# Last head's key tiles: transposed by VectorE and moved through DRAM instead of by TensorE and ScalarE; Pool's two last-head steps swapped; third output block's evacuations spread over four chunks

## The chip, the cores and the metric

One core of one Trainium2 chip runs the whole kernel. The metric is the device time of one execution in microseconds (us). The kernel before took 1402.96 us, the median of 3 runs (1402.95, 1402.96 and 1403.58).

## What is computed

The reference is one inference step of a mixer layer. 640 tokens (128 of context, 512 latent) of 2048 features are normalised, scaled and shifted, and multiplied by one input projection of nine parts of 1024 columns. Eight heads of retention and eight heads of a gated linear recurrence (HGRN2) read the parts, forward and backward, and write final states. Both branches go through one output projection, a gated residual and a last norm. What matters here is how the recurrence's state takes up the keys of a chunk, and the output projection:

```python
s = (jnp.exp(b_last[:, :, 0, :])[..., None] * s
     + jnp.einsum('bhjd,bhjv->bhdv', kc * jnp.exp(b_last - b), vc))
...
out = jnp.concatenate([o_r, o_h], axis=-1).astype(x.dtype) @ w_out
x = x + (gate[:, None, :] * out).astype(x.dtype)
```

The keys times their decay factors are called the factored keys below. The einsum sums over the tokens j, so TensorE needs the tokens of the factored keys on the partitions, while the kernel computes them with the features there: every head's factored keys have to be transposed.

## The kernel before, in words

All loops are written out by hand for five instruction streams (SP issues DMAs, ScalarE is ACT, VectorE is DVE, Pool is GpSimd, TensorE is PE), and semaphores order them: each engine runs its own list from top to bottom, and an instruction whose semaphore isn't there yet holds up all behind it on that engine. Nothing is scheduled by a tool; the written order is the order of the chip.

**Heads.** Each of eight heads streams its input-projection weights in 18 chunks of 512 KB. ACT rounds a chunk to its high part (`split`, L730), DVE makes the low part (L1202), and PE multiplies high by high, high by low and low by high (for token parts L2130 to L2132). The recurrences of head h - 1 are interleaved with the chunks of head h. At the end of a head DVE runs, in `items(17, h, ...)`: the first level's decay differences (`differences`, L1472 and L1474), `boundary_decays` (L1419, L1420), `query_factors` (L1446, twice), `tokens_last` (L1329, which copies two PSUM banks of projected tokens away and so frees them for PE), and `turn_keys` (L1437 to L1439, three transposes of 32x32 blocks). Pool makes the factored keys (`key_factors`, L1824, one 128x1280 product, after ACT's exponentials in L920) and multiplies key decays of a level (`key_decay`, L1847 and L1848, after ACT's exponentials in L879). For heads 0 to 6 the factored keys then go through DRAM: SP's `move_keys` waits for `turn_keys`, writes 512 KB (L536), waits for that, and reads it back in four pieces (L541), which completes the transpose; PE's `chunk_updates` (L2220, L2222) multiplies the result with the values.

**The last head** has no following head, so its recurrences are interleaved with the first block of the output projection. PE's list there is (L2329 on): the first weight chunk for tiles 0 to 3, `level_scores` 0 (L2147), retention updates (L2174, L2175), more of the block, `level_scores` 1, retention outputs (L2186 to L2189), `level_scores` 2, the second weight chunk, and then `key_tokens`: eight 128x128 transposes of the factored keys (L2206, L2208) into two PSUM banks. ACT's `keys` (L863, L864) copies them to `kltok`, PE does the first chunk for tile 4, and `chunk_updates` follows. The first matmul of the block waits for DVE's `tokens_last`, and `level_scores` 3 for DVE's `chunk_states` (L1484, L1486). Pool does `key_decay(last, 0)` before `key_factors(last)`.

**Output projection.** `w_out` is taken in four blocks of 512 columns by 8 chunks; a chunk is split by ACT (L1030) and DVE (L1662) into one of two weight slots, and PE multiplies (L2314 to L2316). A block has five token tiles of 512 columns in five PSUM banks. While block nb runs, DVE evacuates block nb - 1 (`finish`, per tile a gate product L1722 and a residual addition L1729): two tiles after the split of chunk 1 and three after that of chunk 2. ACT then squares a tile (L1064) in each of chunks 3 to 7, and Pool multiplies it by the norm's weights (L1909). In the fourth block (nb = 3) PE does only three of the five tiles in its first pass, so a chunk there is 18 matmuls long and not 30.

Of the kernel before, what the change touches and what calls it, by code (L numbers as in the profile page):

```python
# [41 lines left out]
HEADS = 8  # L42
# [82 lines left out]
def layer(nc, x_prompt, x_sample, s_ret_f, s_ret_b, s_hg_f, s_hg_b, c, c_ctx,  # L125
# [3 lines left out]
    with ctx:  # L129
# [196 lines left out]
        last_keys, pe_hu, pe_level = Signal("last_keys", 2), Signal("pe_hu"), Signal("pe_level", PRODUCTS)  # L326
# [129 lines left out]
        def _(sp):  # L456
# [39 lines left out]
            def store_states(h, new_f, new_b, buf, ready, stored):  # L496
                sp.wait_ge(ready.sem, ready.at(h))
                for s, new in enumerate((new_f, new_b)):
                    sp.dma_start(new[0, 0, bass.ds(h, 1)].rearrange("h d v -> (h d) v"), buf[:, s, :]).then_inc(stored.sem, 16)
# [141 lines left out]
            load_w_out(2)  # L641
            store_states(last, n_ret_f, n_ret_b, rst, r_state, r_state_stored)
# [60 lines left out]
        def _(act):  # L703
# [156 lines left out]
            def keys(h):  # L860

                act.wait_ge(last_keys.sem, last_keys.at(0, 1))
                act.activation(kltok[:, 0:4, :], tiles(ps[:, C, :]), ACT.Copy)  # L863
                act.activation(kltok[:, 4:8, :], tiles(ps[:, DD, :]), ACT.Copy).then_inc(last_keys.sem, 1)  # L864

# [177 lines left out]
            keys(last)  # L1043
# [69 lines left out]
        def _(dve):  # L1113
# [552 lines left out]
            own_decay(last, 0)  # L1666
            split_w(1)
# [114 lines left out]
            for m in range(WCHUNKS, OUT_CHUNKS):  # L1782
                nb, j = m // WCHUNKS, m % WCHUNKS
                split_w(m)
                if nb < OUT_BLOCKS:
                    if j == 1:
                        finish(nb - 1, 0, 2)
                    if j == 2:
                        finish(nb - 1, 2, TILES)
                else:  # L1790

                    if j == 0:
                        finish(OUT_BLOCKS - 1, 0, 1)
                    if j == 1:
                        finish(OUT_BLOCKS - 1, 1, EARLY)
                    if j == 2:
                        early_norm()
                        finish_right(0)
                        finish_left(0)
                        partial_variances()  # L1800
                    if j >= 4:
                        finish_right(j - 3)
# [15 lines left out]
        def _(pool):  # L1818
# [77 lines left out]
            last = HEADS - 1  # L1896
            key_decay(last, 0)
            key_factors(last)
# [18 lines left out]
        def _(pe):  # L1917
# [282 lines left out]
            def key_tokens(h):  # L2200

                pe.wait_ge(h_kl.sem, h_kl.at(h))
                pe.wait_ge(r_S.sem, r_S.at(h))
                pe.wait_ge(r_state.sem, r_state.at(h))
                for i, t in enumerate((0, 1, 2, 3)):
                    nc.tensor.transpose(ps[:, C, tile_cols(i)], KL[:, 0, tile_cols(t)], ident)  # L2206
                for i, t in enumerate((0, 2, 3, 4)):
                    ins = nc.tensor.transpose(ps[:, DD, tile_cols(i)], KL[:, 1, tile_cols(t)], ident)  # L2208
                ins.then_inc(last_keys.sem, 1)

            def chunk_updates(h):

                if h == HEADS - 1:
                    pe.wait_ge(last_keys.sem, last_keys.at(0))
                else:
                    pe.wait_ge(k_moved.sem, k_moved.at(h))
                    pe.wait_ge(r_S.sem, r_S.at(h))
                    pe.wait_ge(r_state.sem, r_state.at(h))
# [125 lines left out]
            pe.wait_ge(r_scaled.sem, r_scaled.at(last))  # L2344
            key_tokens(last)
            pe.wait_ge(h_sT.sem, h_sT.at(last, 3))
            for kk in range(WK):
                first_block(0, kk, shared)
            chunk_updates(last)
# [183 lines left out]
```

## Time and profile before

| what | value |
|---|---|
| median of 3 runs | 1402.96 us |
| the profiled execution's own time | 1402.7 us |
| its span, first to last instruction | 1400.9 us |
| mean granted TensorE clock | 0.998 |
| PE busy | 1384.3 us, 99% |
| DVE, ACT, POOL busy | 1001.1, 483.5 and 367.9 us |
| share of PE in the chain that ended last | 96% |

The span is shorter than the execution's own time by what lies around the first and last instruction (1.8 us). Matmuls overlap: the mean of one is 0.39 us, but one of 512 columns starts every 0.227 us when PE runs without a gap, so gaps are read from the distance of two starts, not from the busy share.

### The profile page before, as it was taken

Reading aid. Unit: us, or ns where it says so; the run is one execution under the profiler, and the core shown is the slowest. Engines: PE = TensorE matmul, PEld = TensorE weight load, DVE = VectorE, ACT = ScalarE, POOL = GpSimd, SP = SyncE. Lnnn points to the kernel's source line nnn. Section 1 sums busy time; section 2 is a strip of 40 time slices with the busy share of each in tenths; the row PEclk is TensorE's granted clock in tenths of the full one; section 3 lists DMA queues with packets and bytes.
Section 4 is the critical chain, followed back from the end, with each engine's and each line's share of the span. In section 5 each row is a group of like instructions: output and inputs, shape, how many; then the busy total and the mean of one; then the engine's idle time right before and its main releaser. Section 6 shows DMA issues by size and latency. Waiting matters only on the chain.

```text
span 1400.9 us, 24706 instructions
## 1 busy us (share of the span) xinstructions
PE 1384.3 (99%) x10042; PEld 1166.2 (83%) x10042; DVE 1001.1 (71%) x1330; ACT 483.5 (35%) x842; POOL 367.9 (26%) x292
## 2 busy tenths in 40 slices
PE   7999999999999999999999999999999999999997
PEld 5788898889888988898889888988898888888886
DVE  5655676667689888988888888877676768532345
ACT  4323243233333333342334333333333344221234
POOL 0000114311532153215321532153206225201220
PEclk9999999999999999999999999999999999999999
DMA  9995443435354535444444444433433357182235
GB/s 388 418 393 184 118 126 71 117 73 140 86 169 114 168 96 175 111 154 119 160 116 140 122 159 126 130 97 106 113 98 85 105 155 274 52 306 94 90 106 210
DMA packets 207735, 212.40 MB, mean 152 GB/s; under 512 B 144256, under 2 KB 156816, under 8 KB 202768
## 3 DMA queue, kind: packets, MB, share of 16 engines
q1 hardware_dynamic: 207600, 210.89, 47.8%
q8 instruction: 79, 1.29, 0.4%
q14 instruction: 24, 0.20, 0.0%
q10 hardware_dynamic: 32, 0.02, 0.0%
HBM read 182.27 MB, written 24.40 MB: 148 GB/s over the span
## 4 chain that ended last, share of the span: by engine, by line
PE 96%; DMA 2%; DVE 1%; SPq 0%; issue 0%; ACT 0%; DVEq 0%; ACTq 0%
PE ps L2130 10%; PE ps L2132 10%; PE ps L2131 10%; PE ps L1968 9%; PE ps L1970 8%; PE ps L1969 8%; PE ps L1944 8%; PE ps L2314 5%; PE ps L2316 5%; PE ps L2315 5%; DMA area<-in_w_mod 2%; PE ps L2147 2%; PE ps L1975 2%; PE ps L1976 2%; PE ps L1977 2%; PE ps L1934 2%
## 5 line engine op out<-in xcount | busy, mean ns | idle before, releaser
L1202 DVE TENSOR_TENSOR w_lo<-area,w_hi 128x1024 fp32r<-128x1024 f32 x143 | 190.4, 1331 | 208.0 <-ACT w_hi L730 207.9
L730 ACT ACTIVATE w_hi<-area 128x1024 fp32r<-128x1024 f32 x143 | 151.5, 1059 | 485.9 <-PE ps L2132 255.7
L2130 PE MATMUL ps<-w_hi,hT_hi 128*128 128x512 f32 x640 | 250.6, 392 | 0.0
L2131 PE MATMUL ps<-w_lo,hT_hi 128*128 128x512 f32 x640 | 249.2, 389 | 0.0
L2132 PE MATMUL ps<-w_hi,hT_lo 128*128 128x512 f32 x640 | 249.1, 389 | 0.0
L1968 PE MATMUL ps<-hT_hi,w_hi 128*128 128x512 f32 x512 | 204.9, 400 | 0.5 <-DVE hT_lo L1262 0.4
L1970 PE MATMUL ps<-hT_hi,w_lo 128*128 128x512 f32 x512 | 199.8, 390 | 0.0
L1969 PE MATMUL ps<-hT_lo,w_hi 128*128 128x512 f32 x512 | 199.8, 390 | 0.0
L2132 PEld LDWEIGHTS ps<-w_hi,hT_lo 128*128 128x128 f32 x640 | 120.2, 188 | 25.2
L2131 PEld LDWEIGHTS ps<-w_lo,hT_hi 128*128 128x128 f32 x640 | 120.2, 188 | 24.6
L2130 PEld LDWEIGHTS ps<-w_hi,hT_hi 128*128 128x128 f32 x640 | 120.2, 188 | 24.6
L1836 POOL TENSOR_TENSOR area<-area 128x320 f32<-128x320 f32 x56 | 49.5, 884 | 320.3 <-PE ps L2147 261.7
L2314 PE MATMUL ps<-w_hi,hT_hi 128*128 128x512 f32 x296 | 116.7, 394 | 0.4 <-DVE w_lo L1662 0.3
L1968 PEld LDWEIGHTS ps<-hT_hi,w_hi 128*128 128x128 f32 x512 | 96.1, 188 | 24.6 <-issue 4.1
L2316 PE MATMUL ps<-w_hi,hT_lo 128*128 128x512 f32 x296 | 115.4, 390 | 0.0
L2315 PE MATMUL ps<-w_lo,hT_hi 128*128 128x512 f32 x296 | 115.3, 389 | 0.0
L1970 PEld LDWEIGHTS ps<-hT_hi,w_lo 128*128 128x128 f32 x512 | 96.1, 188 | 20.8
L1969 PEld LDWEIGHTS ps<-hT_lo,w_hi 128*128 128x128 f32 x512 | 96.2, 188 | 18.5
L1662 DVE TENSOR_TENSOR w_lo<-area,w_hi 128x1024 fp32r<-128x1024 f32 x32 | 42.1, 1317 | 95.6 <-ACT w_hi L1030 95.5
L1460 DVE SCALAR_TENSOR_TENSOR gate_sums<-gate_raw,small,gate_sums 128x512 f32<-128x512 f32 x128 | 102.1, 858 | 3.1 <-DMA gate_raw<-in_w_gate 3.1
L879 ACT ACTIVATE area<-area 128x1280 f32<-128x1280 f32 x56 | 70.6, 1272 | 88.8 <-DVE area L1474 84.4
L1847 POOL TENSOR_TENSOR area<-area 128x320 f32<-128x320 f32 x56 | 67.0, 1197 | 92.7 <-ACT area L879 92.7
(282 smaller groups left out, 2429.1 us busy)
## 6 DMA issues: line engine op xcount, KB each, us to landing
area<-in_w_in SPq DMA_DIRECT2D x144, 512.0 KB, 4.4
area<-in_w_mod SPq DMA_DIRECT2D x26, 1024.0 KB, 12.1
area<-in_w_out SPq DMA_DIRECT2D x38, 512.0 KB, 3.7
gate_raw<-in_w_gate SPq DMA_DIRECT2D x32, 512.0 KB, 4.2
gate_raw<-in_w_mod SPq DMA_DIRECT2D x6, 1024.0 KB, 12.3
o_hi_scratch<-area SPq DMA_DIRECT2D x56, 80.0 KB, 2.4
o_lo_scratch<-area SPq DMA_DIRECT2D x56, 80.0 KB, 2.4
hT_hi<-o_hi_scratch SPq DMA_DIRECT2D x14, 320.0 KB, 7.1
```

The costliest lines, as they stand in the source:

```text
L730: act.activation(split_weights(h, n)[0], raw[:, n % 3, :], ACT.Copy).then_inc(wt_hi.sem, 1)
L1202: v.tensor_tensor(lo, raw[:, n % 3, :], hi.bitcast(F32), ALU.subtract).then_inc(wt_lo.sem, 1)
L1944: ins = mm(ps[:, (banks.start, banks.stop - 1)[s], 0:HALF], wt[:, w], x[:, k, s * HALF:(s + 1) * HALF], start=k == 0 and step == 0, stop=k ...
L1968: mm(ps[:, bank, :], w_hi[:, n % 2, w], hT_hi[:, k, P:T], start=k == 0, stop=False)
L1969: mm(ps[:, bank, :], w_hi[:, n % 2, w], hT_lo[:, k, P:T], start=False, stop=False)
L1970: return mm(ps[:, bank, :], w_lo[:, n % 2, w], hT_hi[:, k, P:T], start=False, stop=k == KT - 1)
L2130: mm(out, hT_hi[:, k, tile_cols(t)], w_hi[:, n % 2, w], start=k == 0, stop=False)
L2131: mm(out, hT_hi[:, k, tile_cols(t)], w_lo[:, n % 2, w], start=False, stop=False)
L2132: i = mm(out, hT_lo[:, k, tile_cols(t)], w_hi[:, n % 2, w], start=False, stop=k == KT - 1)
L2314: mm(out, hT_hi[:, k, tile_cols(t)], hi, start=k == first, stop=False)
L2315: mm(out, hT_hi[:, k, tile_cols(t)], lo, start=False, stop=False)
L2316: return mm(out, hT_lo[:, k, tile_cols(t)], hi, start=False, stop=k == final)
```

## The change

Four edits. DVE turns the last head's keys too: `turn_keys(last)` stands after `own_decay(last, 0)`, ahead of the split of the second `w_out` chunk. SP calls `move_keys(last)` after it has issued the third `w_out` chunk, ahead of the retention states' store. PE's `key_tokens` and ACT's `keys` are gone; `chunk_updates(last)` waits for the DMA like that of the other heads. Pool does `key_factors(last)` before `key_decay(last, 0)`. And DVE evacuates the third output block (nb = 2, during block 3) as two tiles after chunk 1, and one each after chunks 2, 3 and 4. Line numbers of the changed file differ from those of before by up to 16.

```diff
@@ SP @@
             load_w_out(2)
+            move_keys(last)
             store_states(last, n_ret_f, n_ret_b, rst, r_state, r_state_stored)
@@ ACT @@
-            def keys(h):
-
-                act.wait_ge(last_keys.sem, last_keys.at(0, 1))
-                act.activation(kltok[:, 0:4, :], tiles(ps[:, C, :]), ACT.Copy)
-                act.activation(kltok[:, 4:8, :], tiles(ps[:, DD, :]), ACT.Copy).then_inc(last_keys.sem, 1)
...
             decays(last, 2)
-            keys(last)
             split_w(2)
@@ DVE @@
             own_decay(last, 0)
+            turn_keys(last)
             split_w(1)
...
                 if nb < OUT_BLOCKS:
+                    late = nb == OUT_BLOCKS - 1
                     if j == 1:
                         finish(nb - 1, 0, 2)
                     if j == 2:
-                        finish(nb - 1, 2, TILES)
+                        finish(nb - 1, 2, 3 if late else TILES)
+                    if late and j in (3, 4):
+                        finish(nb - 1, j, j + 1)
@@ Pool @@
             last = HEADS - 1
+            key_factors(last)
             key_decay(last, 0)
-            key_factors(last)
@@ PE @@
-            def key_tokens(h):
-
-                pe.wait_ge(h_kl.sem, h_kl.at(h))
-                pe.wait_ge(r_S.sem, r_S.at(h))
-                pe.wait_ge(r_state.sem, r_state.at(h))
-                for i, t in enumerate((0, 1, 2, 3)):
-                    nc.tensor.transpose(ps[:, C, tile_cols(i)], KL[:, 0, tile_cols(t)], ident)
-                for i, t in enumerate((0, 2, 3, 4)):
-                    ins = nc.tensor.transpose(ps[:, DD, tile_cols(i)], KL[:, 1, tile_cols(t)], ident)
-                ins.then_inc(last_keys.sem, 1)
-
             def chunk_updates(h):
 
-                if h == HEADS - 1:
-                    pe.wait_ge(last_keys.sem, last_keys.at(0))
-                else:
-                    pe.wait_ge(k_moved.sem, k_moved.at(h))
-                    pe.wait_ge(r_S.sem, r_S.at(h))
-                    pe.wait_ge(r_state.sem, r_state.at(h))
+                pe.wait_ge(k_moved.sem, k_moved.at(h))
+                pe.wait_ge(r_S.sem, r_S.at(h))
+                pe.wait_ge(r_state.sem, r_state.at(h))
...
             first_block(1, 1, own)
-            pe.wait_ge(r_scaled.sem, r_scaled.at(last))
-            key_tokens(last)
             pe.wait_ge(h_sT.sem, h_sT.at(last, 3))
             for kk in range(WK):
                 first_block(0, kk, shared)
+            pe.wait_ge(r_scaled.sem, r_scaled.at(last))
             chunk_updates(last)
```

Three places of the built programs follow. Nearly every SBUF buffer of the recurrences lies in one tensor, `area`; `ps` is PSUM. On **Pool**, at the end of the loop over the heads, before (L1824 is `key_factors`, L1847 and L1848 are `key_decay`, L1836 and L1837 are `differences`):

```order
L1894 COMPARE_AND_BRANCH
L1847 TENSOR_TENSOR area<-area 128x5x64
L1848 TENSOR_TENSOR area<-area 128x5x64
L1824 TENSOR_TENSOR area<-area 128x1280
L1836 TENSOR_TENSOR area<-area 128x10x32
L1837 TENSOR_TENSOR area<-area 128x10x32
```

and with the change:

```order
L1892 COMPARE_AND_BRANCH
L1822 TENSOR_TENSOR area<-area 128x1280
L1845 TENSOR_TENSOR area<-area 128x5x64
L1846 TENSOR_TENSOR area<-area 128x5x64
L1834 TENSOR_TENSOR area<-area 128x10x32
L1835 TENSOR_TENSOR area<-area 128x10x32
```

The 128x1280 product of the factored keys has moved ahead of the first level's two key-decay products. On **PE**, after the second weight chunk of the first output block, before (L2206 and L2208 are the transposes, L2220 and L2222 are `chunk_updates`):

```order
L2316 MATMUL ps<-w_hi,hT_lo 128x512
L2206 MATMUL ps<-con,area 128x128 x4
L2208 MATMUL ps<-con,area 128x128 x4
L2314 MATMUL ps<-w_hi,hT_hi 128x512
L2315 MATMUL ps<-w_lo,hT_hi 128x512
L2316 MATMUL ps<-w_hi,hT_lo 128x512
L2314 MATMUL ps<-w_hi,hT_hi 128x512
L2315 MATMUL ps<-w_lo,hT_hi 128x512
L2316 MATMUL ps<-w_hi,hT_lo 128x512
L2220 MATMUL ps<-area 128x128 x4
L2222 MATMUL ps<-area 128x128 x4
```

and with the change:

```order
L2300 MATMUL ps<-w_hi,hT_lo 128x512
L2298 MATMUL ps<-w_hi,hT_hi 128x512
L2299 MATMUL ps<-w_lo,hT_hi 128x512
L2300 MATMUL ps<-w_hi,hT_lo 128x512
L2298 MATMUL ps<-w_hi,hT_hi 128x512
L2299 MATMUL ps<-w_lo,hT_hi 128x512
L2300 MATMUL ps<-w_hi,hT_lo 128x512
L2204 MATMUL ps<-area 128x128 x4
L2206 MATMUL ps<-area 128x128 x4
```

Eight transposes have left the list, and nothing has taken their place. On **DVE**, in chunks 1 to 4 of the fourth output block (splits L1662, gate products L1722, additions L1729), before:

```order
L1722 TENSOR_TENSOR area<-ps,area 128x512 x2
L1729 TENSOR_TENSOR area<-area 128x512 x2
L1662 TENSOR_TENSOR w_lo<-area,w_hi 128x1024
L1722 TENSOR_TENSOR area<-ps,area 128x512 x2
L1729 TENSOR_TENSOR area<-area 128x512
L1722 TENSOR_TENSOR area<-ps,area 128x512
L1729 TENSOR_TENSOR area<-area 128x512 x2
L1662 TENSOR_TENSOR w_lo<-area,w_hi 128x1024 x5
```

and with the change:

```order
L1717 TENSOR_TENSOR area<-ps,area 128x512 x2
L1724 TENSOR_TENSOR area<-area 128x512 x2
L1656 TENSOR_TENSOR w_lo<-area,w_hi 128x1024
L1717 TENSOR_TENSOR area<-ps,area 128x512
L1724 TENSOR_TENSOR area<-area 128x512
L1656 TENSOR_TENSOR w_lo<-area,w_hi 128x1024
L1717 TENSOR_TENSOR area<-ps,area 128x512
L1724 TENSOR_TENSOR area<-area 128x512
L1656 TENSOR_TENSOR w_lo<-area,w_hi 128x1024
L1717 TENSOR_TENSOR area<-ps,area 128x512
L1724 TENSOR_TENSOR area<-area 128x512
L1656 TENSOR_TENSOR w_lo<-area,w_hi 128x1024 x3
```

The third tile's evacuation stays behind the split of chunk 2; those of the fourth and fifth tile now stand behind the splits of chunks 3 and 4.

## Rows read from the trace of the kernel before

**Rows 1.** The page, part 4: shares of the span in the chain that ended last.

```profile
PE 96%; DMA 2%; DVE 1%; SPq 0%; issue 0%; ACT 0%; DVEq 0%; ACTq 0%
```

**Rows 2.** Waits of PE from 1140 us to the end: us in total, times, longest.

```profile
PE ps L2314 <- DVE w_lo L1662: 0.3, 1, 0.3
```

**Rows 3.** Timeline of PE around the transposes: start us, us, engine, line, what, count.

```profile
1173.95 0.39 PE L2316 MATMUL ps<-w_hi,hT_lo 128*128 128x512 f32 x1
...
1175.29 0.39 PE L2315 MATMUL ps<-w_lo,hT_hi 128*128 128x512 f32 x1
```

**Rows 4.** Timelines of DVE and PE: the end of `chunk_states`, and `level_scores` 3.

```profile
1182.62 0.34 DVE L1486 SCALAR_TENSOR_TENSOR area<-area,small,ps 128x128 f32<-128x128 f32 x1
...
1183.16 0.56 PE L2147 MATMUL ps<-area 128*32 128x32 f32 x40
```

**Rows 5.** Timelines of POOL and DVE: end of head 6; last row of head 0.

```profile
1012.31 3.30 POOL L1824 TENSOR_TENSOR area<-area 128x1280 f32<-128x1280 f32 x1 [9.95 <-ACT area L920]
...
1012.31 0.48 DVE L1472 TENSOR_TENSOR area<-area 128x320 f32<-128x320 f32 x1
1012.71 3.24 DVE L1474 TENSOR_TENSOR area<-area 128x320 f32<-128x320 f32 x1
...
1017.62 1.22 DVE L1329 COPY area<-ps 128x1024 f32<-128x1024 f32 x1
...
1019.57 0.54 DVE L1439 STREAM_TRANSPOSE area<-area 128x384 f32<-128x384 f32 x1
...
181.64 3.24 DVE L1474 TENSOR_TENSOR area<-area 128x320 f32<-128x320 f32 x1
```

**Rows 6.** Timelines of ACT, DVE and PE at the end of the last head.

```profile
1150.36 1.26 ACT L920 ACTIVATE area<-area 128x1280 f32<-128x1280 f32 x1
...
1152.04 0.48 DVE L1474 TENSOR_TENSOR area<-area 128x320 f32<-128x320 f32 x1
...
1154.78 1.23 DVE L1329 COPY area<-ps 128x1024 f32<-128x1024 f32 x1 [0.51 <-PE ps L2132]
...
1155.71 0.39 PE L2132 MATMUL ps<-w_hi,hT_lo 128*128 128x512 f32 x1
1156.15 0.47 PE L2314 MATMUL ps<-w_hi,hT_hi 128*128 128x512 f32 x1
```

**Rows 7.** Landing times of L536, L541, L631; timelines of SP and ACT between them.

```profile
DMA to landing us min/median/max: 4.9/5.3/5.9
...
1027.55 2.75 SPq L541 DMA_DIRECT2D area<-key_scratch  x4
...
DMA to landing us min/median/max: 2.8/3.6/4.4
...
1166.12 0.43 SPq L631 DMA_DIRECT2D area<-in_w_out  x1
...
1179.93 1.06 ACT L1030 ACTIVATE w_hi<-area 128x1024 fp32r<-128x1024 f32 x1 [0.42 <-PE ps L2316]
...
DMA to landing us min/median/max: 3.5/3.7/11.0
```

**Rows 8.** Timelines of ACT, DVE and PE in the fourth output block.

```profile
1345.54 1.06 ACT L1030 ACTIVATE w_hi<-area 128x1024 fp32r<-128x1024 f32 x1 [3.02 <-PE ps L2316]
...
1347.49 2.32 DVE L1662 TENSOR_TENSOR w_lo<-area,w_hi 128x1024 fp32r<-128x1024 f32 x1
...
1349.13 0.39 PE L2316 MATMUL ps<-w_hi,hT_lo 128*128 128x512 f32 x1
...
1350.19 0.39 PE L2315 MATMUL ps<-w_lo,hT_hi 128*128 128x512 f32 x1
```

**Rows 9.** Windows, start of the kernel: length, busy us by engine, PEclk, DMA share, GB/s.

```profile
5.00:10.00 5.00, 3.29 (x13) 1.92 (x12) 1.81 (x6) 2.81 (x6) 0.00 (x0) 0.82 0.99 391
10.00:15.00 5.00, 5.00 (x17) 2.90 (x16) 2.48 (x3) 4.64 (x8) 0.00 (x0) 0.84 1.00 414
...
25.00:30.00 5.00, 3.36 (x60) 2.48 (x62) 3.52 (x11) 1.20 (x2) 0.00 (x0) 1.00 1.00 416
```

More of the change, by code:

```diff
@@ L325, in layer @@
         h_sq, h_rms, h_gated = Signal("h_sq"), Signal("h_rms", 2), Signal("h_gated")
-        last_keys, pe_hu, pe_level = Signal("last_keys", 2), Signal("pe_hu"), Signal("pe_level", PRODUCTS)
+        pe_hu, pe_level = Signal("pe_hu"), Signal("pe_level", PRODUCTS)
         pe_ho = Signal("pe_ho")
@@ L2198, in retention_columns, with chunk_updates @@
                 nc.tensor.transpose(ctx_columns(following), sT[:, 0:P], ident).then_inc(pe_columns.sem, 1)
-            def key_tokens(h):
-                pe.wait_ge(h_kl.sem, h_kl.at(h))
+            def chunk_updates(h):
+                pe.wait_ge(k_moved.sem, k_moved.at(h))
                 pe.wait_ge(r_S.sem, r_S.at(h))
                 pe.wait_ge(r_state.sem, r_state.at(h))
-                for i, t in enumerate((0, 1, 2, 3)):
-                    nc.tensor.transpose(ps[:, C, tile_cols(i)], KL[:, 0, tile_cols(t)], ident)
-                for i, t in enumerate((0, 2, 3, 4)):
-                    ins = nc.tensor.transpose(ps[:, DD, tile_cols(i)], KL[:, 1, tile_cols(t)], ident)
-                ins.then_inc(last_keys.sem, 1)
-            def chunk_updates(h):
-                if h == HEADS - 1:
-                    pe.wait_ge(last_keys.sem, last_keys.at(0))
-                else:
-                    pe.wait_ge(k_moved.sem, k_moved.at(h))
-                    pe.wait_ge(r_S.sem, r_S.at(h))
-                    pe.wait_ge(r_state.sem, r_state.at(h))
                 for i, t in enumerate((0, 1, 2, 3)):
```

## The prediction

> **What bounds the kernel now.** I read the chain of waits first: PE is 96% of it [rows 1]. Then PE's own waits: from 1140 us on, where all the edits lie, the profile names a single one, 0.3 us in the fourth output block [rows 2]. So an edit gains only what PE no longer executes, plus that wait, and loses whatever PE must newly wait for. The rest of the reading looks for such waits, in the timelines of all engines around the last head's end (1150 to 1190 us) and in the fourth block (1340 to 1355 us).
>
> **TensorE's transposes go.** The reader is to see the distance of two starts: from the last matmul ahead of the transposes (1173.95) to the second one behind them (1175.29) it is 1.34 us [rows 3]; two starts without anything between are 2 x 0.227 = 0.45. PE is the path, nothing covers this: **-0.89 us**.
>
> What is late next? `level_scores` 3 needs DVE's `chunk_states`, which end at 1182.62 + 0.34 = 1182.96; PE starts those scores at 1183.16, and the part that waits is the last fifth of about 0.5 us, so at 1183.56 [rows 4]. That margin is 0.6 us. DVE's list up to there waits for PE's retention outputs, which stand ahead of the transposes, and for nothing behind them, so it doesn't move with PE. PE now asks at 1183.56 - 0.89 = 1182.67; a signal from DVE to a PE start takes 0.14 us (L1329 ends at 1156.01, PE starts at 1156.15) [rows 6]. 1182.96 + 0.14 - 1182.67 = 0.43: **+0.4 us**, between 0 (if DVE gains a little somewhere) and 0.6.
>
> **Pool's key factors first.** In the last head before, ACT's exponentials end at 1150.36 + 1.26 = 1151.62, and Pool does the 128x1280 product only later, so DVE's L1474 at 1152.04 takes 0.48 us [rows 6]. In the heads before it Pool does that product first, as the change has it: it starts 0.3 to 0.4 us before L1474, and L1474 takes 3.24 us, ending about when Pool does (1012.31 + 3.30 against 1012.71 + 3.24) [rows 5]. So it was at the end of all seven heads, the first and the last of which stand there. The two engines hold each other off. With the change the last head's end has their geometry: Pool starts at about 1151.70, L1474 at 1152.04. Behind L1474 the order on DVE is the same as there; L1329 starts 1017.62 - 1012.71 = 4.91 us after it [rows 5], so at 1156.95 in place of 1154.78, and ends at 1158.17. L1329 frees PSUM banks for the first matmul of the output projection, and PE already stands at it now: it starts 0.14 us after L1329, 0.44 after the matmul before [rows 6]. It moves to 1158.31: **+2.16 us**, with nothing on PE to cover it. The upper bound is 2.76 (3.24 - 0.48, if DVE's 0.51 us wait for PE ahead of L1329 didn't absorb some), the lower bound 0, if the product doesn't hold L1474.
>
> The Trainium skill says of that pair ("SBUF — State Buffer", section "SBUF: two separate sides") that Pool and a VectorE instruction with two SBUF inputs share ports under an exclusive lock, which whichever starts first has for its whole length. Taken to the letter, L1472, which has two such inputs and is under way when Pool is released, would keep Pool off for some 0.4 us, and all that follows would be as much later: by the page the sum below would be +1.5. The rows show Pool and L1472 (0.48 us) starting together at 1012.31 and neither longer than elsewhere [rows 5], so I keep 2.16.
>
> L1474 is 2.76 us late for ACT's exponentials of that level as well, and with them for one product on DVE and two on Pool. PE asks for these in `level_scores` 1, which starts at about 1164.3 (the second weight chunk's 24 matmuls end at 1174.2 [rows 3], so start at 1168.5; some 4 us of outputs and scores stand ahead) and now 2.16 later: hidden, 0.
>
> **DVE turns the keys.** In head 6 the three transposes run from the end of L1329 (1018.84) to 1019.57 + 0.54 = 1020.11: 1.27 us [rows 5]. In the new place they follow L1329 (1158.17) and a product of 0.8 us that may be held by Pool, and end at about 1160.5; the split behind them is done by 1162. PE wants it at 1168.5 + 2.16: 0.
>
> **SP moves the keys.** The write is issued at about 1160.6 and lands in at most 5.9, four reads take 2.75 to issue and at most 4.4 to land [rows 7]: 1160.6 + 5.9 + 2.75 + 4.4 = 1173.7. PE asks in `chunk_updates`, which now stand six matmuls behind the second chunk: before, they began at 1175.29 + 5 x 0.227 = 1176.4, now at 1176.4 - 0.89 + 2.16 = 1177.7. Cover 4.0 us: 0. SP is a queue, and all behind `move_keys` waits with it, at most the 1169.3 - 1160.6 = 8.7 us until its last read is issued: the state store, seven pairs of loads for the block's later half, and a `w_out` chunk that goes from 1166.12 to at most 1174.8 [rows 7]. ACT splits that chunk at 1179.93, now 1.27 later, and landing takes 3.7, at worst 11.0: 1178.5, at worst 1185.8. At the median it is hidden by 2.7 us: 0.
>
> **ACT's two copies** go. ACT next waits for PE there: 0.
>
> **Third block's evacuations.** Two of three tiles leave the gap ahead of the split that ran from 1347.49 to 1349.81. PE's starts around it are 1349.13 and, two on, 1350.19: 1.06 where 0.45 is due [rows 8]. With the change the split waits for ACT alone, which ends at 1346.60; even if it takes 2.32 us again it is done at 1349.0, and PE asks at 1349.36. **-0.61 us**, at least -0.4. In chunks 3 and 4, of 18 x 0.227 = 4.1 us each, DVE has room for one tile beside the split.
>
> **Sum:** -0.89 + 0.43 + 2.16 - 0.61 = +1.1 us. The profiled execution took 1402.7 us, so 1403.8; the median of the runs is 0.26 higher, and against it the forecast is **1404.0 us**: no change that a measurement of this kernel can tell (about 0.2%, 2.8 us).
>
> **Rivals.**
> *The clock falls in the new pause.* PE would stand from 1155.94 to 1158.31, 2.37 us. At the start of the kernel two stretches of 5 us hold 1.7 us of idle PE each: in the one the granted clock fell to the lower level, 1.2 GHz of 2.4 (means of 0.82 and 0.84 there and in the next stretch), in the other it stayed at 1.00 [rows 9]. A fall cost 5 x 0.18 + 5 x 0.16 = 1.7 us. For it: the new pause is longer than either. Against it: PE is fully busy on both sides. Time: 1405.7, or 1405.3 if part of the slow stretch falls into the pause. The Trainium skill's page "TensorE: Matmul & The Clock Gate" (What's actually happening) says that the array is throttled by default and only activity releases it, by which a pause endangers the clock; no row here shows a pause of this length.
> *Pool doesn't hold DVE* in the last head: then +2.16 goes and the rest stays, -1.1: 1401.9. For it only that Pool comes out of its loop there; against it seven heads of seven.
> *The keys come late.* This one ends clearly slower. The decisive point is PE at `chunk_updates`, 1177.7: beyond that each us costs one, and 1.7 us late (1179.4) makes the whole slower by 0.2%. If write and reads both landed as slowly as the slowest `w_out` chunk, 11.0 [rows 7], they would be there at 1160.6 + 11.0 + 2.75 + 11.0 = 1185.4, 7.7 us late: 1411.7. Against it: all seven earlier heads landed within the bounds above.
> *The evacuation edit does nothing* (Pool's products hold a split elsewhere): -0.61 goes, 1404.6.
>
> **Chances:** forecast 0.45, clock 0.32, no hold 0.09, late keys 0.06, evacuations 0.08. The range, **1403.0 to 1406.0**, takes in the forecast with its bounds (a half as long stall gives 1402.9, 0.6 us of `level_scores` wait and a stall of 2.76 give 1404.8), the evacuations and the clock; it leaves out no hold and late keys. Slower by over 0.2% (above 1405.8) are late keys and a third of the clock's cases with its bounds added: 0.19. Faster by over 0.2% is no case, 0.02 for what I don't see. Same: 0.79.
>
> **What would show it.** In the profile after: L1474's counterpart near 1152 us at 3.2 us and not 0.5; L1329's counterpart ending near 1158.2; PE's first output-projection matmul near 1158.3 with an idle of some 2 us put down to DVE; the granted clock of 1158 to 1162; no transposes ahead of `chunk_updates`, and the key pieces landing before 1174; a small wait of PE at `level_scores` 3; no wait in the fourth block. The forecast is wrong if L1474 stays at 0.5 us (then faster), if PE idles at `chunk_updates`, or if the clock shows 0.5 behind the pause.

## The result, and the profile after

The changed kernel took **1404.97 us** (median of 22 runs, 1403.51 to 1406.53), the kernel before 1402.80 us (22 runs, 1402.49 to 1404.07): ratio 1.0014, 95% interval 1.0008 to 1.0020. By the 0.2% named in the prediction that is no change; it is a small loss all the same, 2.2 us, and not the 1.1 us of the sum.

The runs of the changed kernel fall into two groups by their mean granted TensorE clock. Ten show 0.998, their median is 1403.79 us; twelve show 0.995 to 0.997, their median is 1405.65. The first group lies where the forecast put the time; the second, but for its fastest run, where the clock rival put it, and two more profiles below show one execution of either kind. That fastest run is the profiled execution itself: 1404.8 us (span 1403.0), 2.1 more than the one of before. Behind the pause its granted clock is 1.00 in every window up to 1390 us; it is lower from 5 to 15 us (0.81 and 0.84) and from 1395 us on (0.74), as in the profile of before (0.82, 0.84 and 0.74).

The page's chain of the changed kernel, which answers to [rows 1]:

```profile
PE 93%; DMA 5%; DVE 1%; ACT 1%; SPq 0%; issue 0%; DVEq 0%; ACTq 0%
```

PE is still the path; DMA's larger share comes from ahead of all the edits, most of it from the start of the kernel. PE's waits from 1140 us on, which answer to [rows 2]: us in total, times, longest.

```profile
PE ps L2298 <- DVE area L1323: 2.3, 1, 2.3
PE ps L2298 <- DVE w_lo L1656: 0.2, 1, 0.2
```

The wait in the fourth block is gone, and two have come: one for `tokens_last` (now L1323), one for a split of weights (L1656). Both can be followed in the timelines. First the end of the last head on POOL, DVE and PE, which answers to [rows 6] (start us, us, engine, line):

```profile
1152.65 3.23 POOL L1822 TENSOR_TENSOR area<-area 128x1280 f32<-128x1280 f32 x1 [11.13 <-ACT area L915]
...
1152.58 0.48 DVE L1466 TENSOR_TENSOR area<-area 128x320 f32<-128x320 f32 x1
1152.98 3.25 DVE L1468 TENSOR_TENSOR area<-area 128x320 f32<-128x320 f32 x1
...
1157.89 1.22 DVE L1323 COPY area<-ps 128x1024 f32<-128x1024 f32 x1
...
1156.55 0.39 PE L2130 MATMUL ps<-w_hi,hT_lo 128*128 128x512 f32 x1
1159.26 0.47 PE L2298 MATMUL ps<-w_hi,hT_hi 128*128 128x512 f32 x1 [2.32 <-DVE area L1323]
```

Pool starts its long product during L1466, and L1468 behind that takes 3.25 us where it took 0.48. `tokens_last` ends at 1159.11, and PE starts 2.71 us after its last projection matmul; before it was 0.44. **The stall costs 2.27 us.**

Then PE's chunk updates and the weight split behind them (PE, then DVE):

```profile
1178.69 1.05 PE L2204 MATMUL ps<-area 128*128 128x128 f32 x8
...
1182.22 0.50 PE L2298 MATMUL ps<-w_hi,hT_hi 128*128 128x512 f32 x1 [0.19 <-DVE w_lo L1656]
...
1179.63 1.00 DVE L1466 TENSOR_TENSOR area<-area 128x320 f32<-128x320 f32 x1
1180.55 0.48 DVE L1468 TENSOR_TENSOR area<-area 128x320 f32<-128x320 f32 x1
1180.95 1.21 DVE L1656 TENSOR_TENSOR w_lo<-area,w_hi 128x1024 fp32r<-128x1024 f32 x1
```

`chunk_updates` began at 1176.45 before (in the fence below) and begin at 1178.69 now, 2.24 later, after PE had come to the stall 0.84 later (1156.55 against 1155.71) and lost 2.27 in it: 0.84 + 2.27 - 2.24 = **0.87 us won** by the transposes' leaving. Six matmuls of the output projection behind the updates, PE stands for the split of the third `w_out` chunk, which DVE has done only at 1182.16. The start of that matmul comes 0.58 after the one before it, and the next one 0.34 after that, where 0.227 each is due: **0.46 us given back**. The same places before (PE, DVE):

```profile
1176.45 1.10 PE L2220 MATMUL ps<-area 128*128 128x128 f32 x8
...
1179.67 0.39 PE L2314 MATMUL ps<-w_hi,hT_hi 128*128 128x512 f32 x1
...
1177.80 1.23 DVE L1662 TENSOR_TENSOR w_lo<-area,w_hi 128x1024 fp32r<-128x1024 f32 x1
```

There the split ended at 1179.03, and PE asked for it at 1179.67.

In the fourth block (DVE), which answers to [rows 8], the splits have 1.2 us again and stand behind nothing but ACT:

```profile
1349.37 1.23 DVE L1656 TENSOR_TENSOR w_lo<-area,w_hi 128x1024 fp32r<-128x1024 f32 x1 [1.52 <-ACT w_hi L1025]
```

No two starts of PE's matmuls in that block are over 0.30 us apart; the gap of 0.61 is gone.

The sum of what the edits did in this profile is 2.27 - 0.87 + 0.46 - 0.61 = +1.25, and with the 0.84 us by which PE was late before any of them, the 2.1 of the two profiles. These 0.84 are no work of the change: the programs are alike up to there, the same changed program starts that matmul at 1155.59 and 1155.92 in two more profiles, and over all the profiles below it starts anywhere from 1155.2 to 1156.9 us.

### The profile page after: what moved, and what is told of

Its sections match the earlier page's. It is cut to its first block, busy times and chain, and to the rows that moved or that the text cites. A ratio compares the mean times of both kernels' runs of the same rounds, so it can differ in the third digit from the quotient of the medians.

```text
span 1403.0 us, 24697 instructions
## 1 busy us (share of the span) xinstructions
PE 1383.5 (99%) x10034; PEld 1165.2 (83%) x10034; DVE 1004.2 (72%) x1333; ACT 482.4 (34%) x840; POOL 368.7 (26%) x292
## 4 chain that ended last, share of the span: by engine, by line
PE 93%; DMA 5%; DVE 1%; ACT 1%; SPq 0%; issue 0%; DVEq 0%; ACTq 0%
PE ps L2128 10%; PE ps L2129 10%; PE ps L2130 10%; PE ps L1966 8%; PE ps L1967 8%; PE ps L1968 8%; PE ps L1942 8%; PE ps L2298 5%; PE ps L2299 5%; PE ps L2300 5%; DMA area<-in_w_mod 3%; PE ps L2145 2%; PE ps L1973 2%; PE ps L1974 2%; PE ps L1975 2%; PE ps L1932 1%
## 5 line engine op out<-in xcount | busy, mean ns | idle before, releaser
L1656 DVE TENSOR_TENSOR w_lo<-area,w_hi 128x1024 fp32r<-128x1024 f32 x32 | 39.9, 1248 | 93.8 <-ACT w_hi L1025 93.7
```

## Experiments

Three questions are open: whether Pool's order alone makes the stall, whether the clock makes the second group of runs, and why the gains of the two other edits are not kept. Medians are set against the median of the runs of before on the same chip. Since the start of the kernel varies, each profile is also read from the start of PE's last projection matmul to the start of its last matmul, the stretch that holds all the edits ("tail"):

| kernel | tail, us | against before |
|---|---|---|
| before | 236.21 | |
| changed, first profile | 237.48 | +1.27 |
| changed, two more profiles | 238.91, 237.37 | +2.70, +1.16 |
| Pool's order undone | 236.07 | -0.14 |
| Pool's order alone | 238.39 | +2.18 |
| evacuations alone | 235.61 | -0.60 |
| PE kept busy in the pause, ten matmuls twice | 239.06 | +2.85 |
| PE kept busy in the pause, once | 237.27 | +1.06 |
| the pause made longer | 241.23 | +5.02 |
| Pool behind, `tokens_last` first | 236.02 | -0.19 |
| ... and the third split first | 236.33 | +0.12 |
| ... and the last order on DVE | 235.40 | -0.81 |

### Pool's order undone

```diff
-            key_factors(last)
             key_decay(last, 0)
+            key_factors(last)
```

> The change with Pool's two steps in their old order (key_decay(last, 0), then key_factors(last)); all else as changed. Theory (the 128x1280 product on Pool holds DVE's second difference, tokens_last comes late, PE stands 2.3 us): DVE's L1468 takes 0.48 us again, PE's first output-projection matmul starts 0.44 us after the last projection matmul as before, the stall of 2.3 us is gone. Keys are turned when Pool's product ends (about 1159.5 on the time axis of before), transposed by 1161, landed by 1173.5 at worst, PE asks at 1175.6: no wait there. The time is before - 0.89 (transposes) + 0.4 (DVE behind PE in w_out chunk 2 or level_scores 3) - 0.61 (evacuations) = -1.1: 1401.7 us against a median of 1402.8, and the runs lie close together as those of before do. Rival A (DVE's turning and the key DMAs cost the time): it stays near 1405. Rival B (keys late without Pool's head start): PE waits at chunk_updates, each us one.

1402.62 us (11 runs, 1402.16 to 1403.57) against 1402.81: ratio 0.9999, interval 0.9990 to 1.0008; tail -0.14 and not -1.1. The stall is gone (PE starts 0.44 us after its last projection matmul), keys are in time, but 0.9 us of the expected gain are missing. PE's waits of this kernel from 1140 us on, and DVE's transposes in its timeline:

```profile
PE ps L2184 <- DVE area L1374: 0.8, 1, 0.8
PE ps L2298 <- DVE w_lo L1656: 0.2, 1, 0.2
```

```profile
1159.65 0.71 DVE L1431 STREAM_TRANSPOSE area<-area 128x512 f32<-128x512 f32 x1 [2.86 <-POOL area L1822]
...
1165.36 0.34 DVE L1374 SCALAR_TENSOR_TENSOR area<-area,small,ps 128x128 f32<-128x128 f32 x1
```

The theory failed in part: the stall went, and the full gain didn't come. Rival B's wait at `chunk_updates` didn't come either; rival A was wrong in its time, but turning the keys does cost. A new wait stands at the retention outputs (L2184), for `retention_chain` (L1374), which is behind `turn_keys` on DVE, and `turn_keys` itself waits 2.86 us for Pool's product here. Read from the starts, the new wait is worth 0.87 us, and the one for the third chunk's split 0.46, as in the changed kernel. In the changed kernel the last L1374 started at 1166.81 and PE asked at 1168.14, with margin to spare, since PE had been held for 2.3 us. The transposes were hidden by the very stall that the other edit made.

### Pool's order alone

```diff
+            key_factors(last)
             key_decay(last, 0)
-            key_factors(last)
```

> The kernel before with Pool's two steps swapped and nothing else. Theory: L1474 takes 3.24 us, PE's first output-projection matmul is 2.2 to 2.3 us later, all else moves with it: +2.2, 1405.0 us, with the runs spread upward by up to 2.5 us as with the change if that spread comes from the new pause. Rival A (turning and DMAs): no change, 1402.8. Rival C (the spread of the change's runs comes from its DMAs, not from the pause): 1405.0 with all runs within 0.5 us.

1406.01 us (9 runs, 1405.08 to 1407.12): ratio 1.0024, interval 1.0014 to 1.0034. L1474 takes 3.24 us, and PE:

```profile
1158.53 0.47 PE L2314 MATMUL ps<-w_hi,hT_hi 128*128 128x512 f32 x1 [2.20 <-DVE area L1329]
```

PE's last projection matmul started at 1155.93, so the stall is 2.60 - 0.44 = 2.16 us. No last-head key was turned by DVE here and no DMA added: the swap makes the stall by itself. The median is 1.0 above the 1405.0 expected; seven of the nine runs have a mean clock below 0.998, where the changed kernel has 12 of 22. The two runs at a clock of 0.998 or more took 1405.08 and 1405.56, the seven below it 1405.99 to 1407.12, so the spread doesn't come from the key DMAs either.

### The evacuations alone

The edit to `finish` in the kernel before, as in the change.

> The kernel before with the third block's evacuations spread over four chunks and nothing else. Theory: the split of chunk 3 no longer stands behind the evacuation of three tiles, PE's gap at 1349 us (0.61) goes: 1402.2 us. Rival (Pool's products hold a split elsewhere, or a later wait takes the gain): within 0.2 of before, 1402.8.

1402.18 us, 11 runs between 1401.95 and 1402.41, against 1402.81 (31 runs from 1402.31 on). The ratio, 0.9996 with interval 0.9987 to 1.0005, can't tell it from no change, but the profile can: the view of PE's waits from 1140 us on is empty, the matmuls of the fourth block follow each other at 0.227 us, and the tail is 0.60 us shorter, the size of the gap that is gone.

### PE kept busy in the pause

```diff
                     pe.wait_ge(tok_act.sem, tok_act.at(last, 1))
+                    for n in range(10):
+                        mm(ps[:, A, :], hT_hi[:, 15, 0:P], hT_hi[:, 15, P:T], start=True, stop=True)
                     pe.wait_ge(tok_dve.sem, tok_dve.at(last))
```

> The change, with ten more 128x512 matmuls on PE right ahead of its wait for tokens_last (into PSUM bank A, which nothing reads then; the output is not touched), so that PE works through most of its 2.3 us pause. The runs of the change lie in two groups, near 1403.75 and near 1405.6 us. Theory clock (the upper group is a fall of the granted clock set off by the pause): all runs near 1403.8, granted clock 0.998 in all. Rival (the upper group has another cause: start of the kernel, DMAs): the two groups stay, median about 1405. If the ten matmuls outlast the pause, they add up to 0.3 us to either.

1405.60 us (11 runs, 1405.18 to 1406.70), ratio 1.0018, interval 1.0009 to 1.0027. The edit did more than was meant: the code around it runs a second time for the chunk's fifth tile, and ten matmuls more stood on PE's path there (2.27 us), of which 0.46 took the place of the wait for the third chunk's split. 1403.79 + 2.27 - 0.46 = 1405.60. So it can be read as a single group, but not well; the tail, 239.06, comes near the same sum (237.37 + 2.27 - 0.46 = 239.18). Therefore once more, in the first call only:

```diff
+                    if 0 in tokens:
+                        for n in range(10):
+                            mm(ps[:, A, :], hT_hi[:, 15, 0:P], hT_hi[:, 15, P:T], start=True, stop=True)
```

> The change with ten more 128x512 matmuls on PE ahead of its wait for tokens_last, this time once only (the earlier kernel issued them a second time, 2.27 us more, ahead of the first chunk's fifth tile); the output is not touched. Theory clock (the upper group of the change's runs is a fall of the granted clock set off by the 2.3 us pause): all runs within 0.5 us of 1403.8, granted clock 0.998 or above but for a run or two. Rival (the upper group comes from the start of the kernel or from the DMAs): the runs spread from 1403.5 to 1406.5 as the change's do, median near 1405.

1403.94 us, all 11 runs between 1403.42 and 1404.28, ten of them at 0.998 or 0.999: ratio 1.0006, interval 0.9997 to 1.0015. Work that changes nothing in the result, put into the pause, brings the median down by a microsecond, since the second group is gone. (The two medians come from separate sessions; the kernel before took 1402.80 and 1402.83 us in them.) The tail is that of the changed kernel with the clock kept (237.27 against 237.37): PE's real work starts again 2.50 us after its last projection matmul, about as late as without the ten matmuls (2.59), and only the clock is saved.

### The pause made longer

```diff
+                if isinstance(h, int) and h == LAST:
+                    v.tensor_copy(gate_sums[:, :, :], ps[:, 2:4, :])
+                    v.tensor_copy(gate_raw[:, 0, 0:2 * WIDE].rearrange("p (b n) -> p b n", b=2), ps[:, 2:4, :])
                 v.tensor_copy(tok[:, 3:5, :], ps[:, 2:4, :]).then_inc(tok_dve.sem, 1)
```

> The change with two more copies of 1.14 us each on DVE right ahead of tokens_last (the same PSUM banks, copied into buffers that nothing reads any more; the output is not touched), so that PE's pause is 4.6 us and not 2.3. Theory clock: the granted clock falls behind the pause in nearly every run, and the profile shows windows below 1.00 between 1160 and 1175 us; 1403.75 + 2.28 + 1.7 to 2 = 1407.7 to 1408.0. Rival (the pause does nothing to the clock): 1406.0 for half of the runs and up to 1408.5 for others, all windows from 1150 to 1390 us at 1.00.

1408.16 us (5 runs, 1407.65 to 1409.68), ratio 1.0040, interval 1.0026 to 1.0054; no run is above a clock of 0.997. Windows of two us of its PE (length, PE busy and instructions, granted clock, DMA share, GB/s):

```profile
1156.00:1158.00 2.00, 0.55 (x3) 1.00 1.04 390
1158.00:1160.00 2.00, 0.00 (x0) 1.00 1.05 398
1160.00:1162.00 2.00, 0.92 (x3) 0.82 1.04 393
1162.00:1164.00 2.00, 2.00 (x6) 0.50 0.61 229
1164.00:1166.00 2.00, 2.00 (x46) 0.83 0.53 215
```

The clock goes to the lower level behind the pause, as the clock theory said; the median is 0.2 above its range. The parts fit: the tail is 3.86 us longer than that of the changed kernel with the clock kept (241.23 against 237.37), 2.33 of it is the longer pause (4.92 us from start to start, 1156.16 to 1161.08, against 2.59), and 1.53 are left for the fall.

### The changed kernel again, twice

No edit; two more executions, profiled.

> The changed kernel again, for another profile of it. Theory clock: if this execution takes over 1405 us, its granted clock is below 1.00 in windows behind PE's pause, between 1157 and 1170 us, with matmuls 0.43 us apart; if it takes under 1404, the clock stays at 1.00 there. Rival: an execution over 1405 us with 1.00 in all windows there, its extra time ahead of 1150 us.

> The changed kernel once more, with the same expectation as the one before it: over 1405 us with a fall of the granted clock behind the pause, or under 1404 without one.

1405.30 and 1404.05 us, one of each group. The slower one (windows, then PE's timeline):

```profile
1156.00:1158.00 2.00, 0.00 (x0) 1.00 1.04 394
1158.00:1160.00 2.00, 1.82 (x6) 0.73 1.04 394
1160.00:1162.00 2.00, 2.00 (x7) 0.50 1.05 396
1162.00:1164.00 2.00, 2.00 (x50) 0.91 0.87 344
```

```profile
1155.59 0.39 PE L2130 MATMUL ps<-w_hi,hT_lo 128*128 128x512 f32 x1
1158.18 0.47 PE L2298 MATMUL ps<-w_hi,hT_hi 128*128 128x512 f32 x1 [2.20 <-DVE area L1323]
1158.49 0.40 PE L2299 MATMUL ps<-w_lo,hT_hi 128*128 128x512 f32 x1
1158.72 0.43 PE L2300 MATMUL ps<-w_hi,hT_lo 128*128 128x512 f32 x1
1158.95 0.63 PE L2298 MATMUL ps<-w_hi,hT_hi 128*128 128x512 f32 x1
1159.38 0.63 PE L2299 MATMUL ps<-w_lo,hT_hi 128*128 128x512 f32 x1
```

and the other (the same views):

```profile
1156.00:1158.00 2.00, 0.31 (x2) 1.00 1.04 392
1158.00:1160.00 2.00, 1.49 (x7) 1.00 1.04 396
1160.00:1162.00 2.00, 2.00 (x48) 1.00 1.04 393
```

```profile
1155.92 0.39 PE L2130 MATMUL ps<-w_hi,hT_lo 128*128 128x512 f32 x1
1158.51 0.47 PE L2298 MATMUL ps<-w_hi,hT_hi 128*128 128x512 f32 x1 [2.20 <-DVE area L1323]
1158.82 0.39 PE L2299 MATMUL ps<-w_lo,hT_hi 128*128 128x512 f32 x1
```

The pauses are alike to the hundredth, 2.59 us from start to start. In the slower execution three matmuls run behind it at the old pace, then the starts lie 0.43 us apart until 1162.4: the clock is at 0.50, 1.2 of 2.4 GHz. In the other it stays at 1.00. The same stretch of PE's list, from the first output-projection matmul to the first one behind `level_scores` 2, takes 1172.21 - 1158.18 = 14.03 us in the one and 1170.98 - 1158.51 = 12.47 in the other: the fall cost **1.56 us**. The slower one reached the pause 0.33 sooner; 1.56 - 0.33 = 1.23 is the difference of the two times but for 0.02. What decides in which execution the clock falls no run shows.

### Repairs on Pool and DVE

Pool's product waits until DVE's two differences are done, and DVE takes `tokens_last` ahead of `query_factors`:

```diff
+            pool.wait_ge(xq.sem, xq.at(last, 1))
             key_factors(last)
...
+                    if isinstance(h, int) and h == LAST:
+                        tokens_last(h)
+                        query_factors(h)
```

> The change with two repairs at the last head's end: Pool's product waits until DVE's two differences are done, and DVE does tokens_last (a copy out of PSUM) ahead of query_factors. Theory (Pool's product holds DVE operations that read two SBUF tiles, not a copy out of PSUM): L1468 0.48 us, tokens_last at the time of before, no stall of PE at its first output-projection matmul; query_factors stretch in its place, which nobody waits for; keys turned by 1160, so no wait at L2184 or at chunk_updates; 0.45 is still lost at w_out chunk 2. Time 1402.8 - 0.89 - 0.61 + 0.45 = 1401.75. Rival (Pool holds every DVE operation): tokens_last waits for Pool's product to end at about 1155.8 and ends at 1157, PE stands 1 us: 1402.7.

1402.12 us (11 runs, 1401.59 to 1402.96) against 1402.83: ratio 0.9995, interval 0.9985 to 1.0004. Its timelines of POOL and DVE:

```profile
1152.19 2.96 POOL L1826 TENSOR_TENSOR area<-area 128x1280 f32<-128x1280 f32 x1 [12.00 <-DVE area L1468]
1155.11 0.87 POOL L1849 TENSOR_TENSOR area<-area 128x320 f32<-128x320 f32 x1
...
1154.30 1.22 DVE L1323 COPY area<-ps 128x1024 f32<-128x1024 f32 x1 [2.03 <-PE ps L2135]
1155.44 2.64 DVE L1440 TENSOR_TENSOR area<-area 128x640 f32<-128x640 f32 x2
```

The copy out of PSUM runs beside Pool's products and takes its 1.22 us; `query_factors`, with two SBUF inputs, takes 2.64 instead of 1.56. PE has no stall at its first output-projection matmul. This is the pair that the Trainium skill names ("SBUF — State Buffer", section "SBUF: two separate sides"): a VectorE instruction with two SBUF inputs against a Pool instruction that reads SBUF, and the traces agree. But the tail is 0.19 us shorter than before, not 1.05: PE's wait at the retention outputs, which I had thought gone, is there again with 0.9. Pool then holds DVE once more: its second product of `differences` had started first, and the split of chunk 1 takes 1.74 us where it takes 1.2 alone.

```profile
1159.95 0.72 POOL L1839 TENSOR_TENSOR area<-area 128x320 f32<-128x320 f32 x1
...
1160.01 1.74 DVE L1660 TENSOR_TENSOR w_lo<-area,w_hi 128x1024 fp32r<-128x1024 f32 x1
```

The 128x1280 product shows that the hold goes both ways. Here it starts with no DVE product of two SBUF inputs under way and takes 2.96 us. In the changed kernel it started 0.07 us into L1466 (0.48 us) and took 3.23; in the kernel before it started 0.07 us into a longer product, and took 3.56:

```profile
1155.99 3.56 POOL L1824 TENSOR_TENSOR area<-area 128x1280 f32<-128x1280 f32 x1
...
1155.92 0.81 DVE L1322 TENSOR_TENSOR area<-area 128x640 f32<-128x640 f32 x1
```

A DVE product 0.33 longer makes Pool's record 0.33 longer. So Pool waits for the DVE product that came first, by some 0.27 and 0.60 us, and the wait shows as a longer record, not as a later start.

Next, DVE's order further down: the third chunk's split ahead of the differences, `chunk_states` ahead of `own_decay(last, 3)`, `retention_gated` behind both.

```diff
-            differences(last, 3)
             split_w(2)
-            retention_gated(last)
-            own_decay(last, 3)
+            differences(last, 3)
             chunk_states(last)
+            own_decay(last, 3)
+            retention_gated(last)
             split_w(3)
```

> As the kernel above, and on DVE the split of w_out chunk 2 ahead of the fourth level's differences, chunk_states ahead of own_decay(last, 3), and retention_gated behind both. Theory (0.45 us are lost since DVE reaches split 2 late, behind a difference that Pool holds): that wait goes and no other of more than 0.1 us takes its place: 1401.3. Rival (level_scores 3 waits in its place, for own_decay(last, 3) or chunk_states): 1401.75 as the kernel above.

1402.97 us (11 runs, 1402.45 to 1403.87): ratio 1.0000, interval 0.9991 to 1.0009. Neither theory: the wait at the split went, and a larger one came at a place that neither had named. PE's waits from 1140 us on:

```profile
PE ps L2200 <- DVE area L1503: 1.1, 1, 1.1
PE ps L2189 <- DVE area L1374: 0.2, 1, 0.2
```

L1503 is the copy of the scores of level 3, now behind `retention_gated`. The wait at the retention outputs (L2189) is 0.2 here and was 0.9 in the kernel above, though DVE's list up to there is the same. This time the split of chunk 1 came first, by 0.01 us, and Pool's product was held:

```profile
1160.46 1.76 POOL L1839 TENSOR_TENSOR area<-area 128x320 f32<-128x320 f32 x1
...
1160.45 1.18 DVE L1660 TENSOR_TENSOR w_lo<-area,w_hi 128x1024 fp32r<-128x1024 f32 x1
```

So which of the two starts first accounts for 0.56 of the 0.7 us between these two profiles, and the size of that wait can differ between executions of one and the same order. In this kernel DVE stood idle for 1.67 us ahead of `chunk_states`, and `retention_gated` fits there. The last order puts it there, and the second chunk's split, which PE asks for only at 1168.5, behind `retention_chain`:

```diff
             turn_keys(last)
-            split_w(1)
             place(last, None, 0)
             differences(last, 1)
             retention_chain(last)
+            split_w(1)
...
             split_w(2)
             differences(last, 3)
+            retention_gated(last)
             chunk_states(last)
             own_decay(last, 3)
-            retention_gated(last)
             split_w(3)
```

> The change with Pool's product behind DVE's two differences, tokens_last ahead of query_factors, the split of w_out chunk 1 behind retention_chain, the split of chunk 2 ahead of the fourth level's differences, retention_gated between those and chunk_states, own_decay(last, 3) behind chunk_states. Theory (once PE no longer stands at tokens_last, DVE's list is the bound from 1160 to 1190 us, since the key transposes' 1.3 us were hidden only by that stall; what can go behind PE's asking has to): no wait at L2184 (0.8 and 0.9 us in the two kernels without the stall), none at chunk 2 (0.45), none at retention_columns (1.1 in the kernel with retention_gated behind): 1401.4 to 1401.7. Rival (DVE's list is too full: any order moves the wait to the next place): 1402.1 to 1402.8.

1401.77 us (11 runs, 1401.55 to 1403.18) against 1402.64 on that chip: ratio 0.9994, interval 0.9985 to 1.0003. Its one wait from 1140 us on:

```profile
PE ps L2200 <- DVE area L1503: 0.4, 1, 0.4
```

So a good part of the lost time could be had by order alone. The transposes and the evacuations are worth 0.87 + 0.61 = 1.48 us, and the tail keeps 0.81 of them. Read from the starts, PE loses 0.6 at that wait and 0.1 in `level_scores` 3. This version has the lowest median of all: 3.2 us under the changed kernel, and 0.9 under the one before, which by the interval isn't told from no change.

## Why the prediction was right, and where it was not

No change by the 0.2% bound was forecast and came, with 1404.97 us inside the range; the point, 1404.0, was 1.0 too low. In part that is luck: one term came out at another place than forecast, one zero held only because of another term, and the median stands between two kinds of executions. The steps:

- **TensorE's transposes**, forecast -0.89: measured -0.87.
- **Pool's key factors first**, forecast +2.16: measured +2.27 in the first profile, +2.15 in each of the two others, +2.16 with the swap alone. L1474's counterpart took 3.25 us. Seven earlier heads had shown the price of this order, and it was paid an eighth time.
- **Third block's evacuations**, forecast -0.61: measured -0.61 in the profile and -0.63 alone.
- **`level_scores` 3**, forecast +0.43: a size that came out (+0.46) at another place. That DVE's list "doesn't move with PE" held: the third chunk's split starts 3.15 us later than before (1180.95 against 1177.80), `chunk_updates` only 2.24. The step that failed is that I followed this list to its end at `chunk_states` and not to the split ahead of it. That split had 0.64 us to spare before, less the 0.14 of a signal, and without the transposes PE asks for it 0.87 sooner: 0.37, measured 0.46. PE, held there, then came to `level_scores` 3 late enough not to wait.
- **DVE turns the keys**, forecast 0: true in the changed kernel, but not for the reason given. The 1.3 us of transposes were covered by the 2.3 us for which PE stood. Without that stall PE waits 0.8 to 0.9 at the retention outputs in two kernels and 0.2 in a third. The step looked at who asks for the split behind `turn_keys`, and not at `retention_chain`, three steps further. The terms of the sum were therefore not independent: undoing the swap gives back 1.2 of the 2.2 us, not all (1402.62 against 1403.79). Without the swap, the profiles show no gain from taking the transposes off PE but a loss: the tail is 236.07 - 235.61 = 0.46 us longer than with the evacuations alone, -0.87 + 0.87 + 0.46. (The medians differ by 0.44, which their intervals can't tell from nothing.)
- **SP moves the keys**, forecast 0: right. The write was issued at 1161.50, the reads until 1168.80, the slowest landing of a read in any head was 5.3 us (of these four 3.9), so 1174.1 at worst against 1178.69.
- **The clock**: given as a rival with 0.32 and 1405.7 or 1405.3. By the runs' times and mean clocks it came in some eleven of 22 executions, and the median of the upper group is 1405.65; the fall cost 1.56 us, the estimate from the start of the kernel [rows 9] was 1.7. The mechanism and the price were right, the chance too low: "PE is fully busy on both sides" spoke against it and did not prevent it. So the median lies between the two cases, 1.0 above the forecast. By its own last line the forecast is wrong where the clock shows 0.5 behind the pause, which the slower of the two further profiles does: it held for about half of the executions, and the range took in both kinds.
- **The Trainium skill's lock to the letter** ("SBUF — State Buffer", section "SBUF: two separate sides"), by which Pool would wait for the first difference: the traces agree with the page, and the prediction misread its rows. Pool's record starts at 1152.65 with L1466 under way (1152.58, 0.48 us), and it is longer, 3.23 us against 2.96 with nothing of the kind under way. The product of 3.30 in [rows 5] had that wait in it already. So the rows' 2.16 was the right term, the +1.5 counted the wait twice, and "neither longer than elsewhere" was wrong: in all seven heads Pool had been held.
- **Two figures that don't close**, without effect: late keys and a third of the clock's cases make 0.06 + 0.11 = 0.17 and not 0.19, and the 1402.9 that the range is said to take in lies just below its end of 1403.0.

## What to carry to other kernels

A price that a loop pays in every iteration is the price that the epilogue will pay once it is written in the loop's order; it stands in the trace before the edit is made. Work moved into another engine's "idle time" is free only up to the first thing behind it that somebody waits for, so follow that engine's list past the new work to every consumer, and do it again without the stall that another part of the same change makes. And a pause of PE can cost more than its length: if it can't be closed, it can be filled: here matmuls that nobody needs, in the pause and only there, gave back a microsecond at the median.

## What was not expected of the hardware

The same program with the same pause (2.59 us from start to start in both) keeps its clock in one execution and loses it in the next. Of most runs only the mean clock is known, which doesn't tell where it fell. It was below 0.998 in 12 of 22 runs of the changed kernel and seven of nine with the swap alone, both with PE idle for this pause; in two and one of 11 with PE busy through it; and in five of five with 4.92 us from start to start. But it was so without any such pause too, in 12 of 73 runs of the kernel before that were taken beside the experiments, and in four of 11 of the first repair, the two fastest among them. So the counts only estimate the falls in the pause. The Trainium skill's page "TensorE: Matmul & The Clock Gate" (What's actually happening) tells of a clock that only activity releases; the runs agree in direction, and show besides that at this length it is a matter of the execution.

A clock fall at the start of the kernel need not cost anything: before it fell to 0.82 and 0.84 there [rows 9] and PE began its last projection matmul at 1155.71; with Pool's order undone it didn't fall in those windows (all at 1.00), and that matmul began at 1155.78. The slower of the two further executions fell there too (0.86 and 0.79), and reached it 0.33 sooner than the other, which did not fall there. But the three profiles that reach it last, at 1156.16, 1156.55 and 1156.88, all have such a fall before 35 us, and the eight without one reach it from 1155.23 to 1155.93; whether the fall made them late no run shows. Behind the pause, where PE is the path, the same kind of fall cost 1.56 us.
